# First residual LayerNorm of a streaming-encoder block: shared root chain for tiles 0 and 1, one tile measured by ScalarE, half-tile statistics, and half an embedding unit moved in front of the last tile

## What is computed

```python
h1 = _layernorm(DN_ALPHA * h + mix, ln1_w[i], ln1_b[i])
moe = _hier_moe(h1, w_router_group[i], b_router_group[i], w_router_expert[i],
                b_router_expert[i], w_exp_gate[i], w_exp_up[i], w_exp_down[i])
ple = jax.nn.sigmoid(h1 @ w_ple_gate[i] + b_ple_gate[i]) * (p[i] @ w_ple[i])
h = _layernorm(DN_ALPHA * h1 + moe + ple, ln2_w[i], ln2_b[i])
...
def _layernorm(x, w, b):
    mu = mean(x); xc = x - mu
    var = mean(xc * xc)
    return xc * lax.rsqrt(var + LN_EPS) * w + b
```

## Time and profile before

| | before |
|---|---|
| median of 3 runs | 796.5 us (796.02 to 796.9) |
| the profiled execution's own time | 796.83 us |
| its span in the trace | 795.0 us |
| PE busy | 736.1 us (93%) |
| DVE busy | 422.8 us (53%) |
| ACT busy | 201.2 us (25%) |
| POOL busy | 183.9 us (23%) |
| mean granted PE clock | 0.966 of full |

### The profile page before, as it was taken

The page is one execution under the profiler, slowest core; times in us unless marked ns, Lnnn a source line. Parts: engine busy times, 40 slices in busy tenths (PEclk is TensorE's granted clock), DMA queues, the critical chain, the costliest instruction groups (busy, mean ns, idle before and its releaser), DMA issues.

```text
span 795.0 us, 9744 instructions
## 1 busy us (share of the span) xinstructions
PE 736.1 (93%) x3799; PEld 519.1 (65%) x3799; DVE 422.8 (53%) x751; ACT 201.2 (25%) x351; POOL 183.9 (23%) x129
## 2 busy tenths in 40 slices
PE   4999999999999999999999999999999989888672
PEld 2897788998887878747888888544544444343220
DVE  6698946775678898663276947511221111021326
ACT  3312424555322323242130240211211111111130
POOL 4924490000032222004060002411111111111242
PEclk9999999999999999999999968999999999999985
DMA  9798132311121122324152496599999999999492
GB/s 308 268 409 196 53 107 60 101 54 54 44 65 54 54 54 54 132 106 158 54 229 90 168 403 223 171 418 419 409 412 418 420 421 419 420 420 415 144 204 107
DMA packets 61816, 173.16 MB, mean 218 GB/s; under 512 B 16982, under 2 KB 39712, under 8 KB 47946
## 3 DMA queue, kind: packets, MB, share of 16 engines
q1 hardware_dynamic: 52324, 141.79, 47.4%
q0 software_dynamic: 8752, 28.59, 11.1%
q10 hardware_dynamic: 694, 2.14, 0.7%
HBM read 155.52 MB, written 24.67 MB: 227 GB/s over the span
## 4 chain that ended last, share of the span: by engine, by line
PE 75%; DMA 11%; DVE 9%; issue 2%; POOL 1%; ACT 1%; SPq 0%; DVEq 0%; POOLq 0%
PE psum L902 34%; PE psum L1252 12%; PE psum L1190 6%; DMA ring<-in_w_exp_up_dram 6%; PE psum L1267 5%; PE psum L1111 3%; DMA ring<-in_w_in_dram 3%; PE psum L1060 2%; PE psum L1080 1%; PE psum L1193 1%; PE psum L1209 1%; PE psum L1010 1%; DMA arena<-y_rows,rowsU 1%; DVE arena L1676 1%; PE psum L979 1%
## 5 line engine op out<-in xcount | busy, mean ns | idle before, releaser
L902 PE MATMUL psum<-ring_r 128*128 128x512 f32 (+1 forms) x928 | 246.6, 350 | 4.1 <-DVE arena_r L1701 1.7
L902 PEld LDWEIGHTS psum<-ring_r 128*128 128x128 f32 x928 | 163.3, 191 | 29.0 <-issue 4.0
L902 PE MATMUL psum<-arena_r,ring_r 128*128 128x512 f32 (+1 forms) x416 | 140.9, 376 | 0.0
L751 POOL TENSOR_TENSOR ring_r<-ring,ring_r 128x2048 fp32r<-128x2048 f32 x16 | 73.8, 4619 | 204.6 <-ACT ring_r L1365 204.6
L1252 PE MATMUL psum<-ring,arena 128*64 128x512 f32 x512 | 114.6, 600 | 4.3 <-DMA ring<-in_w_exp_up_dram 4.3
L1365 ACT COPY arena<-psum 128x512 f32<-128x512 f32 (+4 forms) x104 | 57.3, 581 | 193.9 <-PE psum L1267 56.0
L1252 PEld LDWEIGHTS psum<-ring,arena 128*64 128x64 f32 x512 | 40.0, 138 | 76.2 <-issue 76.2
L902 PEld LDWEIGHTS psum<-arena_r,ring_r 128*128 128x128 f32 x416 | 79.2, 190 | 13.7 <-issue 0.5
L1267 PE MATMUL psum<-ring,arena 128*64 128x512 f32 x256 | 61.0, 619 | 9.2 <-issue 9.2
L1190 PE MATMUL psum<-arena 128*128 128x256 f32 x256 | 65.4, 403 | 1.2 <-DVE rowsU L2133 1.2
L2164 DVE SCALAR_TENSOR_TENSOR arena<-arena,psum 128x256 f32<-128x256 f32 x16 | 9.7, 609 | 105.0 <-ACT arena L1578 105.0
(11 more groups left out here) (299 smaller groups left out, 987.5 us busy)
## 6 DMA issues: line engine op xcount, KB each, us to landing
ring<-in_w_exp_up_dram SPq DMA_DIRECT2D x32, 1024.0 KB, 14.7
ring<-in_w_exp_down_dram SPq DMA_DIRECT2D x32, 1024.0 KB, 13.4
ring<-in_w_exp_gate_dram SPq DMA_DIRECT2D x32, 1024.0 KB, 12.7
ring<-in_w_in_dram SPq DMA_DIRECT2D x18, 1024.0 KB, 5.3
y_rows<-arena POOLq DMA_DIRECT2D x12, 1024.0 KB, 17.0
ring<-in_w_out_ssd_dram SPq DMA_DIRECT2D x4, 1024.0 KB, 7.1
ring<-in_w_out_dram SPq DMA_DIRECT2D x4, 1024.0 KB, 5.0
arena<-in_w_ple_gate_dram SPq DMA_DIRECT2D x4, 1024.0 KB, 15.8
```

Source lines behind the costliest of these rows:

```text
L751: g.tensor_tensor(lo, ring[:, SLOT_OF[seq]], hi.bitcast(F32), ALU.subtract).then_inc(s_w_lo, 1)
L902: t = mm(o, a, b, start=(first and j == 0), stop=(last and j == 2))
```

## The change

Three edits, and one that follows from them.

- DVE, L2001 and `normed`: tiles 0 and 1 are first added in full (four half tiles), DVE measures tile 1, and one `rsqrt` chain works on two columns for both tiles; then both are scaled. Tiles 2 and 3 keep a chain each, but each half's statistics follow its own add.
- ACT measures tile 0 with `tile_stats`, which it uses for two other LayerNorms already, once the tile's two adds are done (`s_mix_read`). DVE waits for it (`s_act_stats`) in front of the chain.
- PE runs `ple_half(0, 0)`, the first half of embedding unit 0, between route 1 and the transposes of tile 3, and no longer behind route 3. No bank moves.
- The last LayerNorm's wait counts one more measurement by ACT.

```diff
@@ -1157,22 +1157,6 @@
                            stop=(k == KD - 1))
                 return t
 
-            for i in range(NT):
-                pe.wait_ge(s_h1_ready, i + 1)
-                o = opened(("h1T", i), D, 2)
-                for k in range(KD):
-                    t = tr(o[:, k * P:(k + 1) * P], h1[:, i, k, :], ident)
-                t.then_inc(s_pe_h1T, 1)
-                if i == 1:
-                    logits = opened("rt", NT * 36)
-                if i:
-                    route(logits, i - 1)
-            route(logits, NT - 1).then_inc(s_pe_rt, 1)
-
-
-            pe.wait_ge(s_wsmall_in, 16 * 4)
-            pe.wait_ge(s_pT_read, 2)
-
             def ple_bank(n):
...
@@ -1194,6 +1178,25 @@
                                start=(k == 0), stop=(k == 1))
                     t.then_inc(s_pe_pl, 1)
 
+            for i in range(NT):
+                if i == NT - 1:
+                    opened(("pl", 0))
+                    ple_half(0, 0)
+                pe.wait_ge(s_h1_ready, i + 1)
+                o = opened(("h1T", i), D, 2)
...
+            route(logits, NT - 1).then_inc(s_pe_rt, 1)
+
+
+            pe.wait_ge(s_wsmall_in, 16 * 4)
+            pe.wait_ge(s_pT_read, 2)
+
...
             for n in range(EARLY):
-                opened(("pl", n))
-                ple_half(n, 0)
+                if n:
+                    opened(("pl", n))
+                    ple_half(n, 0)
                 ple_half(n, 1)
...
@@ -1548,6 +1552,8 @@
             out_part(3)
             mix_part(6)
             mix_part(7)
+            act.wait_ge(s_mix_read, 2)
+            tile_stats(h[:, 0, :], 0, h1_words[:, 0, :])
             for kk in range(2):
                 act.wait_ge(s_pe_pT, kk + 1)
                 copy(pT[:, kk, :], bank(("pT", kk))).then_inc(s_pT_read, 1)
@@ -1663,18 +1669,6 @@
...
-            def normed(x, w, b, out, signal):
-
-                for s in range(2):
-                    link(v.bn_stats(stats[:, 6 * s:6 * s + 6], x[:, 512 * s:512 * s + 512]))
-                link(v.bn_aggr(mv[:, 0:2], stats))
-                link(v.tensor_scalar(mv[:, 2:3], mv[:, 1:2], LN_EPS, None, ALU.add))
-                rsqrt(mv[:, 3:4], mv[:, 2:3], mv[:, 4:5])
-                link(v.scalar_tensor_tensor(x, x, mv[:, 0:1], w, ALU.subtract, ALU.mult))
-                by_k = lambda t: t.rearrange("p (n k) -> p k n", k=KD)
-                v.scalar_tensor_tensor(out, by_k(x), mv[:, 3:4], by_k(b), ALU.mult, ALU.add).then_inc(signal, 1)
-                dve.wait_ge(signal, seen(signal))
...
@@ -1994,15 +1988,41 @@
                 mix_rest(n)
             dve.wait_ge(s_ah_ready, NT)
             dve.wait_ge(s_ln_in, 32)
-            for i in range(NT):
+
+            def mix_added(i, b):
+
+                dve.wait_ge(s_pe_mix, 2 * i + b + 1)
+                hb = h[:, i, 512 * b:512 * b + 512]
+                v.scalar_tensor_tensor(hb, bank(("mix", i, b)), 0.5, hb, ALU.mult, ALU.add).then_inc(s_mix_read, 1)
+                dve.wait_ge(s_mix_read, 2 * i + b + 1)
+
+            def roots(tiles):
+
+                link(v.tensor_scalar(rv[0][:, tiles], mva[:, tiles, 1], LN_EPS, None, ALU.add))
+                rsqrt(rv[1][:, tiles], rv[0][:, tiles], rv[2][:, tiles])
+
+            def h1_normed(i):
+
+                x, by_k = h[:, i, :], lambda t: t.rearrange("p (n k) -> p k n", k=KD)
+                link(v.scalar_tensor_tensor(x, x, mva[:, i, 0:1], A1w, ALU.subtract, ALU.mult))
+                v.scalar_tensor_tensor(h1[:, i], by_k(x), rv[1][:, i:i + 1], by_k(A1b), ALU.mult, ALU.add).then_inc(s_h1_ready, 1)
+                dve.wait_ge(s_h1_ready, i + 1)
+
+            for i in range(2):
+                mix_added(i, 0)
+                mix_added(i, 1)
+            tile_stats(h[:, 1, :], 1)
+            dve.wait_ge(s_act_stats, 2)
+            roots(slice(0, 2))
+            h1_normed(0)
+            h1_normed(1)
+            for i in range(2, NT):
                 for b in range(2):
-                    dve.wait_ge(s_pe_mix, 2 * i + b + 1)
-                    hb = h[:, i, 512 * b:512 * b + 512]
-                    v.scalar_tensor_tensor(hb, bank(("mix", i, b)), 0.5, hb, ALU.mult, ALU.add)\
-                        .then_inc(s_mix_read, 1)
-                    dve.wait_ge(s_mix_read, seen(s_mix_read))
-                normed(h[:, i, :], A1w, A1b, h1[:, i], s_h1_ready)
-
+                    mix_added(i, b)
+                    link(v.bn_stats(stats[:, 6 * b:6 * b + 6], h[:, i, 512 * b:512 * b + 512]))
+                link(v.bn_aggr(mva[:, i, :], stats))
+                roots(slice(i, i + 1))
+                h1_normed(i)
...
-            dve.wait_ge(s_act_stats, 1 + 2)
+            dve.wait_ge(s_act_stats, 2 + 2)
```

More of the change, by code:

```diff
@@ L1195, in ple_half @@
                     t.then_inc(s_pe_pl, 1)
+            for i in range(NT):
[4 more added lines that the diff above has]
+                o = opened(("h1T", i), D, 2)
+                for k in range(KD):
+                    t = tr(o[:, k * P:(k + 1) * P], h1[:, i, k, :], ident)
+                t.then_inc(s_pe_h1T, 1)
+                if i == 1:
+                    logits = opened("rt", NT * 36)
+                if i:
+                    route(logits, i - 1)
+            route(logits, NT - 1).then_inc(s_pe_rt, 1)
+            pe.wait_ge(s_wsmall_in, 16 * 4)
+            pe.wait_ge(s_pT_read, 2)
             def rows_turned_in(p):
```

## The result

The changed kernel takes 789.74 us in the median of 4 executions (789.18 to 790.52), against 796.7 us (796.02 to 797.75): ratio 0.9909, 95% interval 0.9895 to 0.9923. The direction was right, the size was not. Rows and times in them come from one profiled execution of each kernel; that of the changed kernel took 789.76 us.

A forecast was written before the change was run, and what follows sets the result against it. The prediction took the kernel as bound by DVE until tile 3 is ready, then by PE, largely at half clock, up to the first `gate_up`. Sum: 796.83 - 0.33 - 3.15 (earlier rank count) = 793.4 us; range 790.3 to 797.2.

The forecast's parts named there:

- DVE's part: DVE's normalization: one root chain (2.12) and tile 0's statistics (1.70) leave, 3.8 us; tile 3 ready at 455.3.
- Route 1 runs from 453.5 … 3.46 us long, to 457.0: PE after route 0: route 1 starts at 453.5, not 454.18, still takes 3.46 us; the half unit follows from 457.0.
- At half clock … with it they end at 465.65: Tile 3's transposes and routes 2 and 3: 8.65 us at half clock; a 3.5 us full-clock stretch ends them 2.1 us earlier.
- Slice 0 in time by 0.7 us: Half unit's weights: slice 0, asked for at 447.68, lands 8.6 us later at 456.3, ahead of the half unit at 457.0.
- The slow rival: PE's queue before tile 3: the half unit waits for a later slice; landing at 463.8 gives 800.2; chance 0.06.
- From routing to ranks: PE from routing's end at 465.65: 6.92 us of full-clock work, the clock rising at 470.05; rank count at 474.8.
- Behind the ranks, 0: After the rank count everything keeps its distance; any change in the clock's second fall was left at 0.
- third rival: Ahead of `rowsU`: the clock's second fall goes as well, up to 3.0 us more, 790.4; chance 0.14.
- One to one to the end: From the first pair's `gate_up` to the end: time won there passes fully, since the weight stream hangs on it.
- The clock rises and stays: Rival at tile 3's routing: it ends at 464.85 and DVE decides the rank count; 5.0 us, 791.5; chance 0.14.
- The clock does not rise in time: Rival at the half unit: routes end at 469.15, rank count 0.5 earlier to 1.1 later, taken as 796.9; chance 0.14.

The follow-up runs named there:

- e4: The changed kernel with weight slice 0 loaded in two transfers and the half unit waiting for the first alone: 788.81 us, ratio 0.990.
- e9: The kernel before with the shared root chain alone: DVE measures tile 0, the half unit stays behind the routing; 793.21 us, ratio 0.9953.
- e10: The kernel before with eight throwaway 128x256 products ahead of tile 3's transposes: 792.49 us, ratio 0.9947.
- e12: The changed kernel with PE's order as before and DVE measuring tile 3's second half four times more: 796.08 us, ratio 0.9976.
- e6: The kernel before, unchanged, run again for a second profile: 795.39 us.
- e3: The changed kernel, but DVE measures tile 0 itself instead of ACT: 790.77 us, ratio 0.9928.
- e5: The kernel before with four throwaway 128x256 products ahead of tile 3's transposes: 795.2 us, ratio 0.9972.

## Why the prediction was wrong, by its own steps

- **DVE's part** held. 3.8 us were forecast off tile 3's readiness and 3.4 came (459.1 to 455.7). The wait for ACT cost 0.33 us where 0 stood, with 0.2 spare: ACT's end was right (428.4), but DVE started 0.46 us after it, and that way to DVE was not counted. The chain of 128x2 steps takes 2.17 us (428.85 to 431.02) against the 2.12 of one column.
- **"Route 1 runs from 453.5 … 3.46 us long, to 457.0" failed**, and the forecast with it. I took the clock's fall at 453.5 as a property of the program, from one profile. Route 1 ran at full clock and was done at 455.1; it ran at full clock in the second profile of before too. Tile 3's transposes began at 458.0 and not at 460.5: 2.5 us. That is the largest part of the miss.
- **"At half clock … with it they end at 465.65" failed** for the same reason. I looked for how soon the half unit would raise the clock, when the question was whether it let the clock fall at all. Transposes and routes took 4.4 us against the 5.15 forecast: 0.7 us. The half unit took 1.8 against 3.5, which is in the 2.5 above.
- **Slice 0 in time by 0.7 us**: the landing (8.4 us after the issue) was right, but PE, faster than thought, waited 1.1 us for it. The slow rival's mechanism was real at that size and cost at most that; e4 removes it.
- **From routing to ranks** I forecast 9.15 us and 8.6 came. The mechanism was right (half a unit less, part of it at half clock). The three together are the 3.7 us by which the ranks came earlier than forecast (471.07 against 474.8).
- **Behind the ranks, 0** was wrong by 1.2 us at `gate_up` 0: the second stretch of half clock halved. It was the third rival's term, priced at up to 3.0. At `down` 0 it is less: 35.1 us behind the ranks in the first profile of before, 34.3 in the second (whose second stretch is 3.4 us too) and 34.3 in the changed kernel's. So at most 0.7 us of it reach the experts, and against the second profile nothing; e9, e10 and e12, with no second fall, are at 34.1 to 34.3. So the forecast's 0 was nearly right for the end, and the rival's 3.0 was priced on PE alone, where PE waits for DVE's work for the first pair as soon as it comes earlier.
- **One to one to the end** held for the change between the two profiles (7.96 us at `gate_up` 0, 8.0 in the span), and not as a rule. Some versions lose 0.5 to 2 us again in the first pair, where PE then waits for DVE, whose work behind the row numbers does not get shorter; e9's view of waits shows the largest:

```profile
PE psum L1277 <- DVE arena L2181: 2.0, 1, 2.0
```

  And from `down` 0 to the end of the span the profiles take 280.4 us (e6) to 284.1 (e3), though none of the kernels differs there: that much of a single profile's span is chance.

- **The rivals.** "The clock rises and stays" (791.5) was the nearest, and less the 1.2 us that the second fall gave it stands at 790.3, 0.6 us above the measured time; the two had 0.28 together. That it comes so near is in part luck: it has route 1 and the half unit at half clock still, and tile 3's transposes at 460.5. "The clock does not rise in time" fell. The page's statement that I put beside it (the Trainium skill, TensorE: Matmul & The Clock Gate, Part 4: PE-mode transpose, that transposes do not count as activity in the way of matmuls) was not tested by these runs: no kernel here has transposes alone in the place of the half unit.

What stays open: whether the pause ahead of tile 3 alone brings the clock down, or PE's whole light stretch behind `mix` does (no run fills another part of it, such as the 0.9 us ahead of route 0); why an equal pause lets the clock fall in one execution and perhaps not in another (e5's times go from 790.2 to 797.4, and two of e10's ten lie above 796, but only one execution of each has a profile); and what the median of e3 lost.

## What to carry to other kernels

Look at the granted clock beside each engine's pauses before pricing work on either: here closing a pause of 3.4 us with useless work gave 5.0 us, and two edits that each close it do not add. Never take a single profile's time of a clock change as a fixed point; take a second profile of the same kernel; here it would have shown that the fall moves, by 5.5 us, and that half clock in tile 3's routes stays. Where a pause can't be closed with real work, products that are thrown away show in one run what the clock costs.

## What the runs showed that I had not expected

- Eight useless 128x256 products (3.5 us of PE) made the kernel before 5.0 us faster: 797.5 to 792.5.
- The half-clock stretch of before (17.1 us in one profile, 13.7 in the other) is down to 3.4 us in the changed kernel's; mean granted clock of the span rose from 0.966 and 0.972 to 0.978.
- 2.9 us of repeated work on DVE, an engine busy for 53% of the span, cost 6 to 7 us.
